# Row gathers from HBM: each gather of V rows also waits for the landing of the one two back

## The reference, cut to what matters

```python
    def chunk(xc):                                   # 128 tokens
        q = (xc @ w_q).reshape(PEER_CHUNK, PEER_HEADS, 2, PEER_DHALF)
        s = jnp.einsum('thzd,znd->thzn', q, sub_keys)
        ...                                          # top 16 of the pairs of keys: eidx, gate
        act = jax.nn.gelu(jnp.einsum('thkd,td->thk', u[eidx], xc), approximate=False)
        return jnp.einsum('thk,thkd->td', gate * act, v[eidx])
```

## Time and profile before

| | |
|---|---|
| median of 3 runs | 4820.68 us (4819.4 to 4829.26) |
| profiled execution | 4808.93 us, span 4807.2 us |
| PE busy | 2817.3 us, 59% of the span |
| DVE busy | 2672.7 us, 56% |
| POOL busy | 2142.2 us, 45% |
| ACT busy | 727.0 us, 15% |
| DMA, POOL's queue | 1086.75 MB, 60.6% of 16 engines' span |
| DMA, SP's queue | 260.48 MB, 16.1% |
| mean granted TensorE clock | 0.769 of full |

### The profile page before, as it was taken

How to read it: one execution, slowest core, us unless ns; L and a number is a source line. 1 busy time by engine, 2 the same in 40 slices (tenths; PEclk the granted TensorE clock), 3 DMA queues, 4 the chain that set the end, 5 groups by cost and what they waited for, 6 DMA issues and landing times.

```text
span 4807.2 us, 38692 instructions
## 1 busy us (share of the span) xinstructions
PE 2817.3 (59%) x12539; PEld 1506.9 (31%) x12539; DVE 2672.7 (56%) x5503; ACT 727.0 (15%) x1560; POOL 2142.2 (45%) x2214
## 2 busy tenths in 40 slices
PE   3989998667896567666477678433333333332323
PEld 2768876655543222233223233100000000000000
DVE  3761113985412947666845774584584585585442
ACT  2322212434301111222210011000000000000000
POOL 1000031630000356554456556666666666666665
PEclk7999999878998889888788888665655555555656
DMA  6532352015234899999999999999999999999998
GB/s 178 132 103 94 106 158 66 27 42 159 80 128 147 299 370 403 356 323 328 320 366 380 388 364 398 380 368 372 378 362 369 388 366 365 388 368 371 369 368 304
DMA packets 494102, 1349.69 MB, mean 281 GB/s; under 512 B 75816, under 2 KB 152080, under 8 KB 491856
## 3 DMA queue, kind: packets, MB, share of 16 engines
q0 software_dynamic: 298768, 1086.75, 60.6%
q1 hardware_dynamic: 195136, 260.48, 16.1%
HBM read 1281.78 MB, written 65.29 MB: 280 GB/s over the span
## 4 chain that ended last, share of the span: by engine, by line
POOL 18%; DMA 12%; issue 9%; DVE 6%; another core or an unknown queue 4%; PE 2%; DVEq 0%; SPq 0%; ACT 0%; POOLq 0%
POOL ring L1934 9%; POOL ring L1941 9%; DMA ring<-in_peer_u,idx 8%; DVE junkF L2106 3%; DMA ring<-in_peer_v,idxT 3%; PE acc L2152 2%; DMA tok<-y_scr 1%; DMA tok<-na_scr 0%; DVE where L1994 0%; DVE rest L1995 0%; DVE where L1997 0%; PE ps_l L1543 0%; DMA n_scr<-tok 0%; DVE best L1996 0%
## 5 line engine op out<-in xcount | busy, mean ns | idle before, releaser
L2106 DVE CUSTOM_DVE_ANT_0 junkF<-ring,ps_n2F 128x1024 bf16<-128x1024 f32 x1024 | 1249.5, 1220 | 919.6 <-DMA ring<-in_peer_u,idx 739.3
L2152 PE MATMUL acc<-ring,spread 128*32 128x512 f32 x4096 | 796.3, 918 | 1339.5 <-DMA ring<-in_peer_v,idxT 1262.0
L1941 POOL DMA_INDIRECT ring<-in_peer_u,idx x1024 | 977.7, 955 | 956.5 <-DVE idx L2036 480.3
L1934 POOL DMA_INDIRECT ring<-in_peer_v,idxT x1024 | 976.2, 953 | 803.0 <-remote 302.4
L2152 PEld LDWEIGHTS acc<-ring,spread 128*32 128x32 f32 x4096 | 157.4, 144 | 1878.4 <-issue 1861.4
L1543 PE MATMUL ps_l<-lane 128*128 128x512 f32 x1536 | 708.5, 613 | 48.5 <-DMA lane<-n_scr 23.2
L1543 PEld LDWEIGHTS ps_l<-lane 128*128 128x128 f32 x1536 | 293.6, 197 | 436.2 <-issue 428.0
L693 POOL MEMSET colmask<- 128x64 f32 x1 | 0.2, 157 | 490.2 <-POOLq L583 490.2
L635 DVE TENSOR_TENSOR w_z_lo<-w_z,w_z_hi 128x512 fp32r<-128x512 f32 x64 | 41.4, 687 | 215.8 <-ACT w_z_hi L610 163.6
L546 PE MATMUL ps_z<-w_z_hi,n_hi 128*128 128x512 f32 x384 | 152.9, 398 | 9.0 <-DVE w_z_lo L635 9.0
L546 PE MATMUL ps_z<-w_z_lo,n_hi 128*128 128x512 f32 x384 | 152.6, 397 | 0.0
(11 more groups left out here) (294 smaller groups left out, 4384.6 us busy)
## 6 DMA issues: line engine op xcount, KB each, us to landing
lane<-in_peer_wq SPq DMA_DIRECT2D x12, 2048.0 KB
adaB<-in_w_ada SPq DMA_DIRECT2D x16, 1024.0 KB, 5.4
w_z<-in_w_in SPq DMA_DIRECT2D x16, 1024.0 KB
ring<-in_peer_u,idx POOLq DMA_INDIRECT x1024
ring<-in_peer_v,idxT POOLq DMA_INDIRECT x1024
zg_scr<-staged SPq DMA_DIRECT2D x48, 256.0 KB, 2.0
lane<-in_w_out SPq DMA_DIRECT2D x6, 2048.0 KB
ada<-in_w_ada SPq DMA_DIRECT2D x8, 1024.0 KB, 19.5
```

Source lines behind the costliest of these rows:

```text
L1934: pool.indirect_dma_start(v_rows[:, nv % RV, :], None, a["peer_v"][0], bass.IndirectOffsetOnAxis(ap=idxT[:, m % 2, col:col + 1], axis=0)). ...
L1941: pool.indirect_dma_start(u_rows[:, n % RU, :], None, a["peer_u"][0], bass.IndirectOffsetOnAxis(ap=idx[:, i % RI, j:j + 1], axis=0)).then_ ...
L2106: nc.vector.tensor_tensor_reduce(out=junk[:, :], in0=u_rows[:, n % RU, :], in1=ps_n[:, :], scale=1.0, scalar=0.0, op0=ALU.mult, op1=ALU.ad ...
L2152: last = nc.tensor.matmul(acc[q * QUAD:(q + 1) * QUAD, cols], spread[:, c0:c0 + QUAD], v_rows[:, nv % RV, cols], start=(g == 0 and b == 0) ...
```

## The change

`IN_FLIGHT = 2` is new. Each V gather from the third on waits also for the landing of the V gather two before it, on that one's ring semaphore. The wait on `v_used` stands only at V gathers whose number is a multiple of four. U gathers are as they were.

```diff
     RU, RV, RI = 5, 8, 2
+    IN_FLIGHT = 2
...
                             if k == 0:
                                 pool.wait_ge(idxT_done, m + 1)
-                            if nv >= RV:
+                            if nv >= RV and nv % QUADS == 0:
                                 pool.wait_ge(v_used, (nv - RV) // QUADS + 1)
+                            if nv >= IN_FLIGHT:
+                                pool.wait_ge(s_v[(nv - IN_FLIGHT) % RV], 16 * ((nv - IN_FLIGHT) // RV + 1))
                             col = k % QUADS * BATCHES + k // QUADS
                             pool.indirect_dma_start(v_rows[:, nv % RV, :], None, a["peer_v"][0],
```

## The result

The changed kernel takes 5071.47 us, median of 4 runs (5068.11 to 5076.21). The kernel before took 4823.54 us beside it, median of 4 (4819.4 to 4829.26). The ratio is 1.0514, interval 1.0496 to 1.0532: 248 us slower. The profiled execution took 5076.21 us, span 5074.5.

What follows compares the result with a forecast made beforehand. It took gathers at 2.88 us a pair as the pace, DMA needing a backlog for full rate. Terms +192, +97, +28 and zero made +317; on the runs' median, 4820.7 + 319, rounded to 5140 us, range 4830 to 5450.

Steps and rivals of the forecast that it cites:

- main case: Late stretch: a pair of V and U gathers takes 3.0 to 3.5 us; 4950 to 5450 us, chance 0.70.
- The ring's wait at every fourth V costs nothing: POOL before V gathers: the three removed waits of four asked for nothing new, costed at nothing.
- The landing wait closes a loop, P = (1.25 + L) / 2: POOL: wake-up 0.30, issue 0.95 and landing L take two pairs' time; L 5.05 gives 3.15, taken as 3.2 us.
- The extra waits as instructions: POOL before V gathers: one wait each, every fourth two, hidden under standing at the landing; zero, 77 us if uncovered.
- The late stretch: 3000 to 4727 us: 600 pairs at 3.20 instead of 2.88 us, +192 us, bounds -192 and +348.
- Before 3000 us: 1658 to 3000 us: 387 pairs at 0.25 us more each, long PE stalls staying; +97 us, bounds -40 and +232.
- The last 37: Last 37 V gathers, running alone: two in flight, L 3.6, 2.4 us each instead of 1.7; +28 us.
- The signs: Profile after: landing waits before nearly every V, 0.7 to 1 us; 3 us "remote" waits gone; late windows 320 to 335 GB/s.
- Rival A: Late stretch: evened issue never lets the queue run dry, DMA stays at 410 GB/s; -194 us, 4627 us, chance 0.13.
- Rival B: POOL: landing wait only replaces the ring wait, pace 2.86 to 2.9 us; +5 to +60, about 4850 us, chance 0.10.
- Rival C: Every eighth V: its 3.09 us wait stays on top, P 3.46 or above; +608, 5430 us, chance 0.07.

Runs made afterwards that it cites:

- e1: Kernel before with the ring's wait at every fourth V gather only and no landing wait: 4821.03 us, ratio 1.000.
- e10: Changed kernel with the landing wait only at V gathers 387 to 986: 4972.98 us, 1.0668 against the kernel before at 4660.34 us.
- e9: Changed kernel with the landing wait only at V gathers 2 to 386: 4739.63 us, 1.0175 against the kernel before at 4660.34 us.
- e5: Kernel before with four U and nine V slots instead of five and eight, no landing wait: 4831.4 us, ratio 1.0047.
- e2: Changed kernel with three V gathers in flight instead of two: 4845.65 us, 1.0048 against the kernel before.
- e7: Kernel before with V and U gathers of half the bytes (2 KB rows), no landing wait: 4687.44 us, ratio 0.9755.
- e6: Kernel before with the second half of the columns left out of the sums in six of eight batches: 4797.17 us, ratio 0.9981.
- e11: Changed kernel with the landing wait only at the last 37 V gathers: 4692.71 us, 1.0072 against the kernel before at 4660.34 us.
- e8: Changed kernel, two V gathers in flight, with V and U gathers of half the bytes: 4723.45 us, 0.9824 against the kernel before.

## Why the prediction was right

The forecast was 5140 us and slower; it took 5071.47, inside the main case's own range of 4950 to 5450. Point by point:

- **The ring's wait at every fourth V costs nothing**: right, e1 gives 1.000.
- **The landing wait closes a loop, P = (1.25 + L) / 2**: right, and the deciding step. The late pace of 3.16 us is a landing of 5.06 us by the formula, against the 5.05 read from three landings. That they agree to 0.01 is partly luck: e10's V gathers land 5.9 - 0.95 = 4.95 us after their issue, and the rest is a longer wake-up. I then took 3.20 for the slower rate seen in the earlier trace rows. The landings alone, 3.15, would have been better.
- **The extra waits as instructions, put at zero**: mis-sized. I had them hidden under POOL's standing at the landing, but at every fourth V gather the second wait costs its time after the landing, 0.76 us to the next issue instead of 0.26. The mean wake-up is then 0.385 us, and with 4.95 to land the formula gives 3.14, where e10 has 3.15. So this is some 0.04 us a pair over my 0.30, an estimate of 25 us in the late stretch, and it is inside the 5.06 us that the formula gives back.
- **The late stretch**: +192 forecast, +167 measured.
- **Before 3000 us**: +97 forecast, +65 measured, 0.17 us a pair instead of 0.25. The term was mis-sized because I took the long stalls on PE as fixed. POOL's waits for PE before these V gathers fell from 178.0 us in 27 to 68.8 in 5, so part of the landing wait seems to be time that POOL would have stood anyway.
- **The last 37**: +28 forecast, +34 measured, 2.66 us each; by the formula that is a landing of 4.07 us, not the 3.6 of a lone gather.
- **The signs**: the "remote" waits went, as forecast. Of the V gathers after 3065 us 467 of 602 waited for a landing, 1.04 us each. The rate was a little above the 320 to 335 GB/s forecast, and its 2 us windows were less even (270 to 387).
- **Rival A** (evened pace, DMA stays at 410 GB/s) needed a landing under 4.5 us with the wait in place, and DMA gave 335 to 340. It fell. Its claim about the kernel before was sound in one point: e9 shows that a queue that never runs low does hold 405 GB/s. But the landing wait keeps it low. With the skill's 3.2 us (the Trainium skill, "DMA: Bandwidth & Descriptors", "Anatomy of one DMA — SWDGE (gpsimd) path") two gathers back would have been free; the measured landing is 4.95 us with three or four under way, and the measurement decides. That a part of this time overlaps with other transfers is how the prediction reads the rows; the page doesn't say it.
- **Rival B** (nothing but the tail) is what 3 in flight did (1.0048), not 2.
- **Rival C** (the 3 us waits stay on top) fell with the changed kernel's two "remote" waits of 2.0 us together. Its premise was half right: the wait is one for a sum's `v_used`, but for an event that comes long after the sum (e5), and e2, e5 and e7 keep most of it.

**What stays open.** Why `v_used` reaches POOL some 5 us late in the traces of the first two series. It isn't the number of waits on the ring (e1), a V slot (e5) or DMA's rate (e7); less work in the sums halves the number of waits (e6). The late code of e1 shows it in the first series and the same code in e9 and e11 does not in the third, so something outside the kernel has a part. But the kernel has one too: in the first series it is gone with one and two V gathers in flight and there with three and four, and with half rows it is there with two as well (e8). No run tells what it is. The size of the change, 5% here, depends on it: the pace with the landing wait is the same in both series, and the pace without it isn't.

## What to carry to other kernels

A wait for the landing of an earlier transfer is a loop: write down its wake-up, its issues and the landing time as it is with that many transfers under way, and compare the sum with the present pace. Take the landing from transfers in the middle of a stream, not from a lone one or a fixed cost plus bytes, and look whether an instruction with two waits wakes up later than one with a single wait (0.76 against 0.26 us here). A DMA busy share of 0.94 doesn't tell that DMA is full: compare its GB/s with the best short window.

## What was not expected of the hardware

- The rate of 0.524 MB gathers goes on rising with the number under way: 217 GB/s at 1.8, 339 at 3.7, 344 at 4.1, 405 at 6.3. Landing grows at the same time from 4.3 to 8.4 us, issue included.
- Gathers of 2 KB rows instead of 4 KB: at half the bytes (192 GB/s, share 0.66) DMA was busy for two thirds of the time that full rows took, not half (0.97).
- The same kernel took 4808 to 4824 us in two series and 4660 in another, 3% apart. The late stretch without a landing wait differs by waits for a semaphore event that comes some 5 us after the sum it tells of, with PE already at other work.
- A V gather with a second wait in front is issued 0.76 us after the landing that releases it, one with a single wait 0.26 us.
